# A decoder block on TensorE: activation rows of 274 columns in place of 272, and of 1024 bytes in the second gate/up

## What is computed

```
hs = concat(meta, x)                                         # 272 tokens
hs = hs + 0.5 * swiglu(rmsnorm(hs), w_gate, w_up, w_down)    # 2048 -> 5632 -> 2048
hs = hs + token_mixing(rmsnorm(hs))                          # w_in 2048 -> 5120, two causal
                                                             # depthwise convolutions, w_out
hs = hs + 0.5 * swiglu(rmsnorm(hs), w_gate2, w_up2, w_down2)
out = rmsnorm(hs)[:, 16:]                                    # the 256 tokens

def swiglu(h, w_gate, w_up, w_down):
    return (jax.nn.silu(h @ w_gate) * (h @ w_up)) @ w_down
```

## Time and profile before

| | |
|---|---|
| median of 3 runs | 1889.36 us (1889.23 to 1889.37) |
| the profiled execution | 1889.21 us, its span 1887.4 us, 1.8 us outside the span |
| PE busy | 1876.6 us, 99% of the span, 13041 matmuls |
| DVE busy, ACT busy | 1108.5 us (59%), 919.4 us (49%) |
| DMA | 342.26 MB, mean 181 GB/s |

### The profile page before, as it was taken

How to read it: one execution, slowest core, us unless ns; L and a number is a source line. 1 busy time by engine, 2 the same in 40 slices (tenths; PEclk the granted TensorE clock), 3 DMA queues, 4 the chain that set the end, 5 groups by cost and what they waited for, 6 DMA issues and landing times.

```text
span 1887.4 us, 32154 instructions
## 1 busy us (share of the span) xinstructions
PE 1876.6 (99%) x13041; PEld 1773.3 (94%) x13041; DVE 1108.5 (59%) x1212; ACT 919.4 (49%) x1167; POOL 5.9 (0%) x17
## 2 busy tenths in 40 slices
PE   9999999999999999999999999999999999999998
PEld 9999999999999999999999998888888888888886
DVE  7555554455544445368899887555566655544444
ACT  6434333343343444359888665444444444443343
POOL 1000000000000000000000000000000000000000
PEclk9999999999999999999999999999999999999999
DMA  7655555555555555555666566666656666666664
GB/s 222 192 173 174 171 177 170 175 175 170 177 171 175 174 174 177 171 176 169 185 185 182 167 199 186 187 188 187 188 178 189 189 193 192 210 186 188 192 186 135
DMA packets 283357, 342.26 MB, mean 181 GB/s; under 512 B 10639, under 2 KB 223985, under 8 KB 283152
## 3 DMA queue, kind: packets, MB, share of 16 engines
q1 hardware_dynamic: 282672, 340.44, 58.6%
q10 hardware_dynamic: 320, 0.53, 0.1%
q0 software_dynamic: 288, 0.19, 0.0%
HBM read 339.02 MB, written 2.10 MB: 181 GB/s over the span
## 4 chain that ended last, share of the span: by engine, by line
PE 99%; DVE 1%; DMA 0%; ACT 0%; issue 0%; SPq 0%; DVEq 0%
PE ps L459 20%; PE ps L461 20%; PE ps L460 20%; PE ps L466 17%; PE ps L467 9%; PE ps L558 4%; PE ps L559 4%; PE ps L560 4%; PE ps L575 0%; DVE w_lo L857 0%; DMA m_rows<-in_meta_tokens 0%; PE ps L421 0%; DVE zc L1056 0%; PE ps L441 0%; DVE ln_mu L881 0%; PE ps L481 0%
## 5 line engine op out<-in xcount | busy, mean ns | idle before, releaser
L857 DVE TENSOR_TENSOR w_lo<-raw,w_hi 128x1024 fp32r<-128x1024 f32 x639 | 781.5, 1224 | 670.8 <-ACT w_hi L634 668.8
L634 ACT ACTIVATE w_hi<-raw 128x1024 fp32r<-128x1024 f32 x639 | 676.1, 1059 | 864.9 <-PE ps L461 519.6
L459 PE MATMUL ps<-x_both,w_hi 128*128 128x272 f32 (+2 forms) x2048 | 590.4, 288 | 1.2 <-DVE x_both L864 1.2
L461 PE MATMUL ps<-x_both,w_lo 128*128 128x272 f32 (+2 forms) x2048 | 589.4, 288 | 0.0
L460 PE MATMUL ps<-x_both,w_hi 128*128 128x272 f32 (+2 forms) x2048 | 586.9, 287 | 0.0
L466 PE MATMUL ps<-x_both,w_hi 128*128 128x512 f32 x1408 | 491.9, 393 | 0.0
L467 PE MATMUL ps<-x_both,w_lo 128*128 128x256 f32 x1408 | 394.9, 280 | 0.0
L459 PEld LDWEIGHTS ps<-x_both,w_hi 128*128 128x128 f32 x2048 | 385.2, 188 | 1.5 <-DVE w_lo L1078 1.4
L460 PEld LDWEIGHTS ps<-x_both,w_hi 128*128 128x128 f32 x2048 | 385.9, 188 | 0.1
L461 PEld LDWEIGHTS ps<-x_both,w_lo 128*128 128x128 f32 x2048 | 385.2, 188 | 0.0
L466 PEld LDWEIGHTS ps<-x_both,w_hi 128*128 128x128 f32 x1408 | 264.3, 188 | 60.3
(11 more groups left out here) (137 smaller groups left out, 1152.9 us busy)
## 6 DMA issues: line engine op xcount, KB each, us to landing
raw<-in_ffn_w_up SPq DMA_DIRECT2D x176, 512.0 KB, 3.6
raw<-in_ffn_w_down SPq DMA_DIRECT2D x176, 512.0 KB, 4.3
raw<-in_ffn_w_gate SPq DMA_DIRECT2D x175, 512.0 KB, 3.8
raw<-in_w_in SPq DMA_DIRECT2D x80, 512.0 KB, 3.6
raw<-in_w_out SPq DMA_DIRECT2D x32, 512.0 KB, 4.7
x_tok<-in_x SPq DMA_DIRECT2D x4, 512.0 KB, 8.3
gain_tok<-in_final_norm SPq DMA_DIRECT2D x1, 1024.0 KB, 6.1
out_y<-o_tok SPq DMA_DIRECT2D x2, 512.0 KB, 2.9
```

The source lines that it names most:

```text
L459: pe.matmul(dst, w_high, act_high, start=first, stop=False)
L461: return pe.matmul(dst, w_low, act_high, start=False, stop=last)
L634: act.activation(w_hi[s][:, :], raw[s][:, :], ACT.Copy).then_inc(hi_ready, 1)
L857: dve.tensor_tensor(w_lo[s][:, :], raw[s][:, :], w_hi[s][:, :].bitcast(F32), ALU.subtract).then_inc(lo_ready, 1)
```

## The change

All places in SBUF at which activations for PE lie in rows of 272 get rows of 274 words (1096 bytes, two words unused), and the regions grow to match: x_region by 2*16*2*4 = 256 bytes, a_region by 2*44*2*4 = 704 bytes. All that lies behind them, the weight buffers first, begins 960 bytes later. The activations of gu2 get a view of their own on x_region, `x2_both`, with rows of 256 words (1024 bytes) that hold only the 256 columns in use. The third row of `step` is given up for space, and the one intermediate of the inverse root that stood there goes to the second row of `sq`. Instructions, their shapes, their number, their order and their waits stay as they were on all engines; only addresses differ.

```diff
+    ROW = T + 2
...
-        sb("x_region", [P, 2 * KD * T])
-        x_at = nc.sbuf_base - 4 * 2 * KD * T
-        sb("a_region", [P, 2 * KF * T])
-        a_at = nc.sbuf_base - 4 * 2 * KF * T
+        sb("x_region", [P, 2 * KD * ROW])
+        x_at = nc.sbuf_base - 4 * 2 * KD * ROW
+        sb("a_region", [P, 2 * KF * ROW])
+        a_at = nc.sbuf_base - 4 * 2 * KF * ROW
...
-        step = sb("step", [P, 3, T])
+        step = sb("step", [P, 2, T])
...
-        x_both = at("x_both", x_at, [P, 2, KD, T], F32R)
+        x_both = at("x_both", x_at, [P, 2, KD, ROW], F32R)[:, :, :, ALL]
         x_hi, x_lo = x_both[:, 0, :, :], x_both[:, 1, :, :]
+        x2_both = at("x2_both", x_at, [P, 2, KD, SEQ], F32R)
...
-        a_both = at("a_both", a_at, [P, 2, KF, T], F32R)
+        a_both = at("a_both", a_at, [P, 2, KF, ROW], F32R)[:, :, :, ALL]
...
                                     m = wide_product(bank, w_hi[s][:, cols], w_lo[s][:, cols],
-                                                     x_both[:, :, k, toks], x_hi[:, k, toks],
+                                                     x2_both[:, :, k, :], x2_both[:, 0, k, :],
                                                      k == 0, k == KD - 1)
...
-                dst = x_hi[:, t, toks]
+                dst = x2_both[:, 0, t, :] if phase == "gu2" else x_hi[:, t, toks]
                 act.activation(dst, res[:, t, toks], ACT.Copy,
                                scale=param(gain_of[norm], t)).then_inc(xhi_ready[norm], 1)
...
-                dve.scalar_tensor_tensor(x_lo[:, t, toks], res[:, t, toks], param(gain_of[norm], t),
-                                         x_hi[:, t, toks].bitcast(F32), ALU.mult,
+                high, low_part = ((x2_both[:, b, t, :] if phase == "gu2" else x_both[:, b, t, toks])
+                                  for b in (0, 1))
+                dve.scalar_tensor_tensor(low_part, res[:, t, toks], param(gain_of[norm], t),
+                                         high.bitcast(F32), ALU.mult,
                                          ALU.subtract).then_inc(xlo_ready[norm], 1)
...
                     inverse_root(ln_rstd[:, :], step[:, 0, 0:SEQ], step[:, 1, 0:SEQ], ln_mu[:, :],
-                                 step[:, 2, 0:SEQ], ln_sd, ln_newton)
+                                 sq[:, 1, 0:SEQ], ln_sd, ln_newton)
...
                             inverse_root(rstd[:, toks], step[:, 0, toks], step[:, 1, toks], sq[:, 0, toks],
-                                         step[:, 2, toks], sd_ready[norm], newton[norm])
+                                         sq[:, 1, toks], sd_ready[norm], newton[norm])
```

## The result

The changed kernel takes 1896.28 us in the median of 5 runs (1896.18 to 1902.4), the kernel before 1889.25 us (1889.23 to 1889.37): a ratio of 1.0048, 95% interval 1.0038 to 1.0059, so slower, by less than 1%. Two of the five runs lie 4 and 6 us above the others, which is why the ratio is above that of the medians, 1.0037; the profiled execution took 1896.28 us, and what follows is about the 7.0 us between the medians.

What follows compares the result with a forecast made beforehand. The prediction took the kernel as bound by PE's matmul pace, which hangs on operand addresses. Terms gu2 -5.8, out_cf -0.9, down2 -2.3 and the rest 0 summed to -9.0 us: 1880.4 us against the median of 1889.36, range 1868 to 1894.

Steps and rivals of the forecast that it cites:

- two streams disturb each other in memory: All matmuls: moving operand and next weight load, read at once, disturb each other when they meet, so distance counts.
- The term for out_cf: out_cf: distance 64 where it was 0, so -2.4 ns by 384 matmuls, -0.9 us.
- the same list of triples: gu1: triples averaged 381.4, 374.4, 382.3 and 374.9 ns for places 0, 64, 128, 192; used as prices.
- down2: down2, weights moving: distance 192 where it was 0, so -2.2 ns by 1056 matmuls, -2.3 us.
- gu2: gu2: distance 64 for all k, 345.1 against 349.2 ns, -4.1 ns by 1408 pairs, -5.8 us.
- cv and b: Stages cv and b: they go through all places as before, 0 us.
- out_sc: out_sc: same matmuls as out_cf, but PE waits near its end for DVE's layernorm, so nothing counted.
- Rival C: Whole stages: kinds only share out an excess whose sum is fixed, so no effect, 1889.4 us; chance 0.10.
- gu1, down1, ag: These 272-column stages, 7104 matmuls: mean over all places unchanged, 0 us, bounds -9.2 to +9.2 us.
- rival B: Half of 7104 matmuls begin at an odd multiple of 8, each losing 2.6 ns, +9.2 us, total 1889.6; chance 0.15.
- rival D: gu1, down1, ag: new rows and shifted low rows bring the cheap kind, -9.2 us more, 1871.2; chance 0.15.
- rival A: Activation's own place counts, not distance: gu2 +5.3 us, out_cf and down2 gain nothing, 1894.7 us; chance 0.15.

Runs made afterwards that it cites:

- all64: Kernel before with 64 unused bytes ahead of everything, so all operands move together and all distances stay: 1889.40 us, one run.
- a_a192: Changed kernel with down2's activations (and `gu2_lo` behind them) 192 bytes later, at the place where its weights stand: 1889.53 us.
- w64: Kernel before with 64 unused bytes ahead of the weight buffers, putting the weights at place 64: 1886.22 us, one run.
- w192: Kernel before with 192 unused bytes ahead of the weight buffers, activations where they were: 1893.65 us, ratio 1.0024.
- d128: Kernel before (rows of 272) with weights at place 128 and gu2's rows of 1024 bytes at place 0: 1897.04 us, one run.
- x276: Kernel before with rows of 276 words for inputs of gu1, ag, cv, b, gu2's runs included; weights at place 0: 1888.74 us.
- low128: Kernel before with low rows of gu1, ag, cv, b inputs 128 bytes further; gu2's and out's rows at place 32, down2's at 224: 1888.78 us.
- a_w0: Changed kernel with 64 more unused bytes ahead of the weight buffers, so weights begin at place 0 again: 1887.06 us, ratio 0.9989.
- off8: Kernel before with inputs of gu1, ag, cv, b 8 bytes later; rows of gu2, out, down2 16 bytes later: 1896.41 us, one run.
- d192: Kernel before (rows of 272) with weights at place 64, gu2's rows at 0, down2's activations at 32: 1896.52 us, one run.

## Why the prediction was wrong

**What held.** The kernel is bound by the pace of matmuls and nothing else: no wait appeared between the stages, and no operation of DVE or ACT mattered. The pace hangs on addresses, and, at places that are multiples of 64, on the distance between the two operands, not on a place: all64 and a_a192 show both. The runs don't show why; that two streams disturb each other in memory was the prediction's ground, and no run measured it. The term for out_cf, -0.9 us, came out as -0.85. That is luck: the same list of triples would have given +0.3 ns at distance 128 and -2.2 at 192, where out_cf then showed -1.3 and -6.7.

**The step that failed: down2.** The prediction put it as "distance 192 where it was 0: 374.9 for 381.4, -2.2 ns by 1056 matmuls, -2.3 us". Measured: +6.5 ns, +6.9 us, and that is nearly the whole result: 1889.2 + 6.9 = 1896.1. The price came from gu1's triples, 272 columns of activations past loaded weights, and was carried to matmuls of 512 columns with the roles of the operands exchanged. Distance 192 is dear there, as it is in gu2's pairs (+6.6), and cheap in out_cf (-6.7). The bounds given for it, "nothing, and twice this", had no loss in them at all, although no row of before showed down2 at any distance but 0. Of the 16 us between the forecast's -9.0 and the +7.0 that came, down2 has 9.2, gu2 5.5, cv and b 1.8; out_sc gave 0.6 back.

**gu2**, -5.8 us predicted, -0.3 measured. The distance is 64 for all k as planned, and the pairs take 349.0. The prediction took 345.1 from those pairs that had distance 64 among others. The runs with one distance for all k give 346.7 for distance 0 (16 and 32 too), 349.0 for 64, 351.1 for 128 and 353.3 for 192 (240 too).

**Under both: a kind's mean was taken for its price.** The prediction read "the same order in every block". In the kernel before, the pairs of k = 0, 1, 2, 3 in gu2 take 346, 348, 354, 357 ns with j = 0 and 344, 350, 345, 348 with j = 1 (means over the stage's start times, k counted modulo 4): the same distance costs 354 or 345. In w64 the same eight values follow each other in the same order, moved along so that some stand at the other j, so that it isn't j. In gu1 the triples of distance 0, 64, 128, 192 take 382, 374, 382, 375 ns before (means without the first group, whose order is another), and 374, 377, 381, 381 in w192, where the dearest kind has become the cheapest while the stage's length is the same to 0.02 us. And in d128 the pairs differ at one single distance. So an interval hangs on the matmuls before it as well, and only a whole stage's mean is a price. Rival C, that the kinds only share out an excess whose sum is fixed, is right for gu1 when the weights move by 64, 128 or 192 (126.1 ns in all four), and wrong for out_cf, gu2 and down2.

**out_sc**, nothing predicted, -0.6 us measured. The prediction let the wait near its end take up the gain; that wait, for `w_lo`, stayed at 0.5 us.

**gu1, down1, ag**, 0 predicted, +0.3, -0.2, 0.0 measured. Right, but as a balance: rival B, the odd multiple of 8, is real (as a start or as a distance), at 1.2 to 2.2 ns for each matmul of gu1 that starts there, where the prediction put 2.6; for half of 7104, if down1 and ag pay the same, that is 4 to 8 us. The finer steps and the shifted low rows give something of the kind back, as x276 and low128 show for gu1 (-0.8 and -0.5 ns). That was rival D in part, and in gu1 the two about cancelled; that they add up is argued, and for down1, whose rows no run moved by themselves, nothing separates them.

**cv and b**, 0 predicted, +1.1 and +0.7 us: "cv and b go through all places as before" left out that they too get odd multiples of 8, and here the finer steps cost as well, so that nothing is given back (in a_w0, with the weights at place 0, +2.1 and +1.6 ns). For b it also left out the order. With rows of 272, b and down1 go through all four distances wherever the weights stand, yet weights at 64 or 192 make b 1.2 to 1.3 ns slower and down1 0.7 faster, and weights at 128 change neither. The loops fit this: `single_group` (b, down1) takes two neighbouring rows in turn for four banks and then the next two, so that distances 0 and 64 alternate, then 128 and 192, or else 64 and 128, then 192 and 0; a move by 64 or 192 exchanges the two cases, one by 128 does not. The first case is the dearer one in both stages (118.7 against 117.5 ns, 126.0 against 125.3). In gu1, ag and cv, where all four follow each other, every move leaves the pace as it was. No run changes the order alone, so this is argued, from five runs.

Two slips of the sums change nothing: 7.0 ns by 3 is 2.3, not 2.4, and 3.7 ns by 1408 is 5.2 us, not 5.3 (so rival A's time is 1894.6).

The Trainium skill's page TensorE: Matmul & The Clock Gate, section "Step-by-step: what each phase is for", has it that loading the next weights takes no read bandwidth from the running matmul; the prediction drew from this that the change would be worth nothing. The trace disagrees with what was drawn: in a_a192 the address of the loaded operand alone moves the running 512 columns by 6.5 ns. Whether it does so through read bandwidth no run shows. The Trainium skill's page SBUF — State Buffer, section "Specifications (TRN2)", has lines of 16 bytes with a penalty at each new one; this agrees in direction with off8, as far as the start and not the distance is what costs there.

## What to carry to other kernels

When a kernel is bound by back-to-back matmuls, as this one is, an allocation is part of the tuning: a buffer that grows moves all behind it, and the loss can fall in a stage that the change never names. So compare the stages' matmul counts per window, those of untouched stages first. Give each stage a view with its own offset and choose its distance to the weights by a run, since neither the best distance nor its sign carries over from one width or from one role of the operands to another; and do not price a stage by the mean of one kind out of a mixed sequence, nor count on the order of the loops to be neutral.

## What was not expected of the hardware

Mean ns from start to start by the distance between moving and loaded operand, all at a granted clock of 1.00 (2.4 GHz):

| distance, bytes | 0 | 16 | 32 | 64 | 128 | 192 | 240 |
|---|---|---|---|---|---|---|---|
| out_cf (256 columns) | 120.0 | 116.7 | 117.8 | 117.8 | 118.7 | 113.3 | 117.1 |
| gu2, a pair (two runs of 256, then 256) | 346.7 | 346.7 | 346.7 | 349.0 | 351.1 | 353.3 | 353.3 |
| down2 (512 columns) | 226.8 | 226.7 | 233.3 | 228.9 | 232.4 | 233.3 | 230.8 |

At one column per cycle of 2.4 GHz, as the prediction counts, the columns themselves are an estimated 106.7, 320.0 and 213.3 ns. So the excess of one matmul goes from 6.7 to 13.3 ns in out_cf and from 13.4 to 20 in down2. It is the same to 0.02 ns when both operands move by 64 bytes (all64), and in down2 at distance 32 for two different pairs of places (d192, low128). The lowest and highest values of the three rows are 17 and 18, 52 and 53, 34 and 35 times 6.67 ns, which is 16 cycles of 2.4 GHz, so that the ends of a row differ by one such step for a matmul or a pair. What takes the step no run shows. Why 32 is as dear in down2 as 192 while gu2 does not notice it, and why out_cf has its best where the others have their worst, stays open: no run shows a single matmul's reads.
